# A decoder stack in float32: half of the second feed-forward matrix by Strassen's scheme, woven with tiles of the first

## The chip, the cores and the metric

The kernel runs on one NeuronCore of a Trainium2 chip. The metric is the device time of one execution in microseconds; the median of three runs of the kernel before is 2151.79 (2151.78 to 2152.73). TensorE (PE) multiplies, ScalarE (ACT) and VectorE (DVE) prepare operands and take results out of the accumulator banks (PSUM), GpSimd (POOL) and SyncE (SP) mostly issue transfers.

## The reference

Two hybrid attention layers, then one block of attention, convolution and feed-forward, on 256 rows of 2048, all in float32. The change concerns only the end of the last block:

```
f = rms_norm(h, g_ffn_pre)
f = square(relu(f @ w_ff1)) @ w_ff2      # w_ff1: 2048 x 8192, w_ff2: 8192 x 2048
h = h + rms_norm(f, g_ffn_post)
```

## The kernel before

Each float32 operand is split into a high part rounded to the matmul's float32r and a low part, the rest. A product is three matmuls: high by high, low by high, high by low. Weights come in blocks of 512 KB through a ring of four (`raw`, filled by SP); ScalarE rounds each block (`high`, L934, `round_block`) and VectorE subtracts (`low`, L490, `low_part`), `RING` blocks deep, so both work a few blocks ahead of TensorE.

TensorE's order is a numbered list of blocks made by `plan`: the feed-forward stage is 256 of them from `FF0` on. It has four quarters. A quarter is eight chunks `f1` of 256 hidden units (four blocks each, weights stationary, rows `xhl` moving, hidden tiles come out transposed) and then four chunks `f2` of 512 output columns (eight blocks each, hidden tiles stationary, weights moving). `weight_block` issues a block: eight matmuls of 512 and eight of 256 columns for `f1` (L682, L699), twelve of 512 for `f2` (L686, L687, L702). Two chunks use the four `acc` banks in turn.

ScalarE and VectorE run beside this by slots (`slots`, `ff_side`), a handful of tasks hung on block numbers. Of a finished `f1` chunk ScalarE copies the crossed half (L954, `cross_out`), VectorE adds it (L1300, `fold`), ScalarE takes relu, square and the rounded copy (L1242, L1244, L1246, `relu_square`), VectorE the low part (L1820). Of an `f2` chunk VectorE adds the banks into `mixed` (L1635, `ff_sum`). The squares of `x` that the norm of the rows needs (L1034, `squares`) hang on slots 10, 12, 14 and 16, two at a time.

The first two chunks of `f1` are interleaved block by block, since their rows are still being transposed (`h2T`, L606); L1792 makes the low part of those rows and counts `xt_ready`, 40 at the last. The last four blocks are done for one half of the rows and then the other, so that the norm of the first half runs under the second.

## Time and profile before

| | |
|---|---|
| median of three runs | 2151.79 us |
| the profiled execution, its span | 2150.6 us |
| around the span (median less span) | 1.2 us |
| TensorE busy | 2125.1 us (99%) |
| VectorE busy | 1361.9 us (63%) |
| ScalarE busy | 1106.1 us (51%) |
| mean granted TensorE clock | 0.999 of 2.4 GHz |

Busy time of matmuls is modelled and overlaps, so the time of a matmul is read from the distance between starts, not from its duration. The feed-forward stage takes about 710 us, a third of the span.

### The profile page before, as it was taken

To read this page: it belongs to the slowest core of one execution; us is meant where nothing else is said; L and a number is where in the kernel's file an instruction comes from. 1 tells how busy PE (TensorE), PEld (TensorE's weight loads), DVE (VectorE), ACT (ScalarE), POOL (GpSimd) and SP (SyncE) were. 2 spreads that over 40 slices of the span, in tenths; PEclk is the share of its full clock that TensorE was granted. 3 is DMA by queue.
4 is the path that set the end of the run, shared out by engine and by line. 5 is a ranking of instruction groups with operands and counts; after the bars stand their busy time and mean duration, and the time that the engine had idled before them with its cause. 6 is when DMAs were issued, how large, how long until landed. Compare 5 with 4: busy or idle time off the path is not lost. (4 is left out here: it accounts for less than half of the span.)

```text
span 2150.6 us, 29240 instructions
## 1 busy us (share of the span) xinstructions
PE 2125.1 (99%) x11602; PEld 1841.8 (86%) x11602; DVE 1361.9 (63%) x1979; ACT 1106.1 (51%) x1541; POOL 156.2 (7%) x78
## 2 busy tenths in 40 slices
PE   8999999999999999999999999999999999999998
PEld 7888888888988888888888888888888888888886
DVE  5554568875577558876578678766555555555555
ACT  4444554454464555555455455656435534544543
POOL 0000000000000000000007873000000000000000
PEclk9999999999999999999999999999999999999999
DMA  8666545655576655655656654646666666666664
GB/s 278 196 189 187 165 138 174 179 172 186 185 214 186 178 148 159 174 167 176 191 180 198 193 178 151 215 136 206 193 193 190 189 193 193 189 194 190 192 190 145
DMA packets 325031, 395.17 MB, mean 184 GB/s; under 512 B 20848, under 2 KB 252912, under 8 KB 324128
## 3 DMA queue, kind: packets, MB, share of 16 engines
q1 hardware_dynamic: 323104, 383.21, 59.0%
q0 software_dynamic: 1792, 10.10, 1.2%
q8 instruction: 92, 1.51, 0.3%
q14 instruction: 43, 0.35, 0.1%
HBM read 391.16 MB, written 2.10 MB: 183 GB/s over the span
## 5 line engine op out<-in xcount | busy, mean ns | idle before, releaser
L490 DVE TENSOR_TENSOR low<-raw,high 128x1024 fp32r<-128x1024 f32 (+2 forms) x672 | 809.9, 1209 | 639.0 <-ACT high L934 635.3
L934 ACT ACTIVATE high<-raw 128x1024 fp32r<-128x1024 f32 (+2 forms) x732 | 763.0, 1046 | 775.8 <-PE acc L682 201.7
L682 PE MATMUL acc<-xhl,high 128*128 128x512 f32 x3198 | 766.4, 391 | 0.0
L682 PEld LDWEIGHTS acc<-xhl,high 128*128 128x128 f32 x3198 | 587.0, 188 | 113.8 <-issue 0.7
L699 PE MATMUL acc<-xhl,low 128*128 128x256 f32 x3200 | 436.9, 286 | 1.9 <-DVE xhl L1792 1.4
L699 PEld LDWEIGHTS acc<-xhl,low 128*128 128x128 f32 x3200 | 414.4, 191 | 18.1 <-DVE xhl L1792 1.8
L686 PE MATMUL acc<-high,yhl 128*128 128x512 f32 (+1 forms) x1036 | 380.1, 373 | 2.2 <-DVE work L1718 1.6
L687 PE MATMUL acc<-high,yhl 128*128 128x512 f32 (+1 forms) x1036 | 378.8, 372 | 0.0
L702 PE MATMUL acc<-low,yhl 128*128 128x512 f32 (+1 forms) x1036 | 241.9, 374 | 0.2
L686 PEld LDWEIGHTS acc<-high,yhl 128*128 128x128 f32 x1036 | 195.2, 188 | 36.8 <-DVE work L1718 2.0
L687 PEld LDWEIGHTS acc<-high,yhl 128*128 128x128 f32 x1036 | 195.2, 188 | 33.8
L702 PEld LDWEIGHTS acc<-low,yhl 128*128 128x128 f32 x1036 | 182.9, 189 | 33.7 <-DVE yhl L1401 1.0
L490 POOL TENSOR_TENSOR low<-raw,high 128x1024 fp32r<-128x1024 f32 x61 | 147.9, 2437 | 81.2 <-ACT high L934 80.9
L1300 DVE TENSOR_TENSOR acc<-acc,cross 128x512 f32<-128x512 f32 x103 | 71.5, 694 | 37.2 <-ACT cross L954 37.0
L1682 DVE SCALAR_TENSOR_TENSOR tb<-work,params,tb 128x256 f32<-128x256 f32 x232 | 93.7, 480 | 0.0
L966 ACT ACTIVATE sc<-sc,small 128x128 f32<-128x128 f32 x64 | 28.6, 448 | 93.0 <-DVE small L1376 92.9
L686 PE MATMUL acc<-high,xhl 128*128 128x512 f32 (+2 forms) x224 | 73.7, 341 | 0.1
L687 PE MATMUL acc<-high,xhl 128*128 128x512 f32 (+2 forms) x224 | 73.1, 339 | 0.0
L702 PE MATMUL acc<-low,xhl 128*128 128x512 f32 (+2 forms) x320 | 72.7, 360 | 0.0
L954 ACT ACTIVATE cross<-acc 128x512 f32<-128x512 f32 x104 | 60.4, 581 | 1.9 <-PE acc L682 1.9
L702 PEld LDWEIGHTS acc<-low,xhl 128*128 128x128 f32 x320 | 53.7, 188 | 8.5 <-issue 1.3
L686 PEld LDWEIGHTS acc<-high,xhl 128*128 128x128 f32 x224 | 42.3, 189 | 5.2 <-issue 0.7
(228 smaller groups left out, 1286.9 us busy)
## 6 DMA issues: line engine op xcount, KB each, us to landing
raw<-in_w_in SPq DMA_DIRECT2D x328, 512.0 KB, 3.7
raw<-in_w_ff SPq DMA_DIRECT2D x256, 512.0 KB, 3.9
raw<-in_w_out SPq DMA_DIRECT2D x91, 512.0 KB, 4.3
raw<-in_w_mem_kv SPq DMA_DIRECT2D x32, 512.0 KB, 5.0
raw<-in_w_in SPq DMA_DIRECT2D x16, 256.0 KB, 2.7
raw<-in_w_out SPq DMA_DIRECT2D x10, 256.0 KB, 2.8
x_nat<-in_mem SPq DMA_DIRECT2D x4, 512.0 KB, 7.8
x_nat<-in_x POOLq DMA_DIRECT2D x4, 512.0 KB, 6.4
```

Of the source, the lines that this page charges most:

```text
L490: eng.tensor_tensor(part(low, g), part(raw, g), part(high, g).bitcast(F32), ALU.subtract).then_inc(ready, 1)
L682: ins = pe.matmul(acc[:, 2 * (c.acc % 2) + s, :], wh[:, t, at], vhl, start=first, stop=last)
L686: pe.matmul(outs[s], vh[:, at], wh[:, t, :], start=first, stop=False)
L687: ins = pe.matmul(outs[s], vl[:, at], wh[:, t, :], start=False, stop=last)
L699: ins = pe.matmul(acc[:, 2 * (c.acc % 2) + s, S:2 * S], wl[:, t, at], vh, start=crossed and t == 0, stop=last)
L702: ins = pe.matmul(outs[s], vh[:, at], wl[:, t, :], start=False, stop=last)
L934: act.activation(part(high, g), part(raw, g), ACT.Copy).then_inc(high_ready, 1)
L954: act.activation(cross, crosses(c), ACT.Copy).then_inc(cross_ready, 1)
L966: ins = act.activation(sc[:, j % 2, s, 0:n], src, ACT.Exp, bias=nmx[:, r:r + 1], accum_out=rs[:, r:r + 1])
L1300: dve.tensor_tensor(out, accs(c), cross, ALU.add).then_inc(folded, 1)
L1682: ins = dve.scalar_tensor_tensor(out=cv[:, ct, :] if tap == TAPS - 1 else sums_at, in0=src, scalar=w, in1=sums_at, op0=ALU.mult, op1=ALU.add)
```

## The change

The first 1024 of the 2048 columns of `w_ff2` are multiplied by Strassen's scheme in Winograd's form for 28 of the 32 pairs of hidden tiles: a pair (256 hidden units by 256 rows) and the matching 256 x 1024 weights are 2 x 2 blocks each, and seven products of 128 x 128 by 128 x 512 replace eight. The sums before it are made in float32 and then split in high and low: three sums of the weights (`group_sums`), four of the hidden tiles (`pair_sums`). A product keeps its own bank over four pairs (`RUNS` runs of four); then VectorE adds the seven banks to sums in memory (`sums_out`), and after the last run mixes these (`mix_sums`). The other 1024 columns, and all 2048 for the last four pairs, are taken in blocks as before (`piece`).

The first matrix is taken in 64 tiles of 128 hidden units, two blocks each (`feature_tile`), and the order is a new list, `FF_ORDER`: the high products of a group (14 matmuls), a tile, the low products (7), a tile; after four groups eight pieces. All seven product banks are busy, so every tile from the fifth on goes to the one bank `obank`, and ScalarE copies it out (`tile_copy`) before the next may start. VectorE folds, and takes relu and square in one operation of two halves (`relu_of`). Low parts of the blocks are written over the raw weights, so a load may start only when TensorE has used the block four before it. The groups' weights have two buffers of their own (`bset`), loaded by SP when the low products release them. The division by the row norm leaves the sum and appears in the last epsilon.

```diff
-    for q in range(NQ):
-        f1 = [("f1", q, j) for j in range(8)]
-        if q == 0:
-            run(*[chunk(k, a["w_ff1_2"][0], D * q + 256 * j, width=256, flipped=True) for j, k in enumerate(f1[:2])])
-        for j, k in enumerate(f1):
-            if q or j >= 2:
-                flip(k, a["w_ff1_2"][0], D * q + 256 * j)
-        for n, (col, width) in enumerate(FCOLS):
-            add(("f2", q, n), a["w_ff2_2"][0], col, width=width, row0=D * q)
+    w = a["w_ff1_2"][0]
+    run(*[chunk(("f1", 0, j), w, 256 * j, width=256, flipped=True) for j in range(2)])
+    w2 = a["w_ff2_2"][0]
+    for kind, *at in FF_ORDER:
+        if kind == "tile":
+            add(("g1", at[0]), w, P * at[0], width=P, nk=8)
+        elif kind == "piece":
+            e, n, i = at
+            if i == 0:
+                chunk(("f2", e, n), w2, CW * n, row0=8 * P * e, kts=8)
+            place(by["f2", e, n], i)
...
+TILES, TILES_AHEAD = 64, 4
+GROUPS, RUNS = 28, 7
+BESIDE = {0: (6, 7), 1: (None, 8), 2: (9, 10), 3: (None, 11)} | {j: (2 * j + 4, 2 * j + 5) for j in range(4, GROUPS)}
+def ff_order():
+    yield from (("tile", 4), ("tile", 5))
+    for j in range(GROUPS):
+        yield ("high", j)
+        if BESIDE[j][0] is not None:
+            yield ("tile", BESIDE[j][0])
+        yield ("low", j)
+        yield ("tile", BESIDE[j][1])
+        if j % 4 == 3:
+            yield from (("piece", j // 4, n, i) for n in (2, 3) for i in range(4))
+    for i in range(2):
+        for n in range(2):
+            yield ("piece", RUNS, n, i)
+            yield ("tile", 60 + 2 * i + n)
+    yield from (("piece", RUNS, n, i) for i in (2, 3) for n in range(2))
+    yield from (("piece", RUNS, n, i) for n in (2, 3) for i in range(4))
+FF_ORDER = list(ff_order())
+FF1 = FF0 + 8
...
+            def feature_tile(n):
+                if n > TILES_AHEAD + 1:
+                    pe.wait_ge(tile_out, n - TILES_AHEAD)
+                    if n - 12 in range(0, 56, 8):
+                        pe.wait_ge(piece_out, 4 * ((n - 12) // 8) + 3)
+                bank = tile_bank(n)
...
+            def group_high(j):
+                pe.wait_ge(pair_ready, j + 1)
+                pe.wait_ge(split_high, 3 * j + 3)
+                for p, unit, n in PRODUCTS:
+                    if j % 4 == 0:
+                        product_released(j // 4, p)
+                    for hl in range(2):
+                        pe.matmul(bank_of[p], rows_of(hl, j, n), bset_r[:, j % 2, 7 + unit, :], start=j % 4 == 0 and hl == 0,
+                                  stop=False)
+            def group_low(j):
+                pe.wait_ge(split_low, 3 * j + 3)
+                for p, unit, n in PRODUCTS:
+                    ins = pe.matmul(bank_of[p], rows_of(0, j, n), bset_r[:, j % 2, unit, :], start=False, stop=j % 4 == 3)
+                ins.then_inc(group_used, 1)
...
+            def tile_copy(n):
+                act.wait_ge(block_used, last_of(("g1", n)))
+                if n >= TILES_AHEAD + 2:
+                    act.wait_ge(pair_sq, n // 2)
+                act.activation(tcopy[:, n % 2, :], tile_bank(n), ACT.Copy).then_inc(tile_out, 1)
...
+            def ff_period(j):
+                n, b = next_blocks(j), BESIDE[j][0] is not None
+                p = {0: 2, 1: 3, 2: None, 3: 4}[j] if j < 4 else j + 1 if j % 4 else None
+                if j < 4 or j % 4:
+                    tile_copy(BESIDE[j - 1][1] if j else 5)
+                if b:
+                    round_block(n[2])
+                if j + 1 < GROUPS:
+                    split_h(j + 1, 0)
+                if b:
+                    round_block(n[3])
+                if j + 1 < GROUPS:
+                    split_h(j + 1, 1)
+                    split_h(j + 1, 2)
+                if b:
+                    tile_copy(BESIDE[j][0])
+                if p is not None:
+                    pair_h(p)
+                m = n[4:6] if b else n[2:4]
+                round_block(m[0])
+                round_block(m[1])
+                return m[1] + 1
...
+            cross_out(("f1", 0, 0))
+            round_block(FF1 + 2)
+            round_block(FF1 + 3)
+            cross_out(("f1", 0, 1))
+            split_h(0, 0)
+            pair_h(0)
+            split_h(0, 1)
+            split_h(0, 2)
+            round_block(FF1 + 4)
+            tile_copy(4)
+            round_block(FF1 + 5)
+            pair_h(1)
+            for c in range(4):
+                x_squares(c)
+            for j in range(GROUPS):
...
+            for b, task in enumerate((None, None, None, None, None, 60, None, None, 61, 30, None, None, 62, None, None, 63)):
+                if b >= 2:
+                    round_block(g + b)
+                if task in (60, 61, 62, 63):
+                    tile_copy(task)
+                if task == 63:
+                    pair_h(31)
+                if b == 10:
+                    pair_h(30)
...
+            def relu_of(pair, v):
+                if pair:
+                    dve.wait_ge(pair_ready, pair)
+                for t in range(2):
+                    ins = dve.scalar_tensor_tensor(out=combo[:, 2 * t:2 * t + 2, :].rearrange("p s n -> p (s n)"), in0=v[:, t], scalar=0.0,
+                                                   in1=v[:, t], op0=ALU.max, op1=ALU.mult)
+                ins.then_inc(pair_sq, 1)
...
+            def group_sums(g):
+                units = bset[:, g % 2]
+                dve.wait_ge(group_landed[g % 2][0], 16 * (g // 2 + 1))
+                dve.tensor_tensor(units[:, 1, :], units[:, 1, :], units[:, 0, :], ALU.subtract).then_inc(sum_step, 1)
+                dve.wait_ge(group_landed[g % 2][1], 16 * (g // 2 + 1))
+                dve.wait_ge(sum_step, 3 * g + 1)
+                dve.tensor_tensor(units[:, 4, :], units[:, 3, :], units[:, 1, :], ALU.subtract).then_inc(sum_step, 1)
+                dve.wait_ge(sum_step, 3 * g + 2)
+                t2 = units[:, 4, :].unsqueeze(1).broadcast_to([P, 2, CW])
+                dve.tensor_tensor(units[:, 5:7, :], t2, units[:, 0:3:2, :], ALU.subtract).then_inc(sum_step, 1)
+            def split_l(g, part_no):
+                dve.wait_ge(sum_step, 3 * g + 3)
+                dve.wait_ge(split_high, 3 * g + part_no + 1)
+                at, end = ((2, 4), (0, 2), (4, 7))[part_no]
+                dve.tensor_tensor(bset_r[:, g % 2, at:end, :], bset[:, g % 2, at:end, :], bset_r[:, g % 2, 7 + at:7 + end, :].bitcast(F32),
+                                  ALU.subtract).then_inc(split_low, 1)
...
+            def ff_period(j):
+                n, b = next_blocks(j), BESIDE[j][0] is not None
+                p = {0: 2, 1: 3, 2: None, 3: 4}[j] if j < 4 else j + 1 if j % 4 else None
+                if j == 3:
+                    fold_pair(p)
+                if j + 1 < GROUPS:
+                    group_sums(j + 1)
+                if p is not None and j != 3:
+                    fold_pair(p)
+                if b:
+                    low_block(n[2])
+                if p is not None and p < 4 * RUNS:
+                    pair_sums(p)
+                if b:
+                    low_block(n[3])
+                if j + 1 < GROUPS:
+                    for part_no in range(3):
+                        split_l(j + 1, part_no)
+                if j % 4 == 3:
+                    sums_out(j // 4, OUTS[:3])
+                if p is not None:
+                    pair_l(p)
+                m = n[4:6] if b else n[2:4]
+                low_block(m[0])
+                low_block(m[1])
+                return m[1] + 1
...
+            def piece_run(e, g):
+                p = 4 * e + 5
+                sums_out(e, OUTS[3:5])
+                low_block(g)
+                sums_out(e, OUTS[5:7])
+                fold_pair(p)
+                low_block(g + 1)
+                if p < 4 * RUNS:
+                    pair_sums(p)
+                low_block(g + 2)
+                pair_l(p)
+                low_block(g + 3)
+                pieces_out(e, 2)
+                for b in (4, 5, 6):
+                    low_block(g + b)
+                pieces_out(e, 3)
+                low_block(g + 7)
...
+            for b in range(2, 16):
+                low_block(g + b)
+                if b == 3:
+                    mix_sums()
+                if b == 9:
+                    fold_pair(30)
+                if b == 10:
+                    pair_l(30)
+            fold_pair(31)
+            pair_l(31)
...
+                if g >= FF1 + RING:
+                    sp.wait_ge(block_used, g - RING + 1)
...
+            def load_group(j):
+                if j < 2:
+                    sp.wait_ge(xt_ready, 40)
+                else:
+                    sp.wait_ge(group_used, j - 1)
+                for t in range(2):
+                    r0 = P * (2 * j + t)
+                    dst = bset[:, j % 2, 2 * t:2 * t + 2, :].rearrange("p a b -> p (a b)")
+                    sp.dma_start(dst, a["w_ff2_2"][0][r0:r0 + P, 0:2 * CW]).then_inc(group_landed[j % 2][t], 16)
```

ScalarE where the feed-forward stage begins, before: the crossed half of the second chunk, relu, square and rounding of the first, and the first squares of `x` between weight blocks.

```order
L954 ACTIVATE cross<-acc 128x512 [waits folded,block_used]
L934 ACTIVATE high<-raw 128x1024 [waits block_used,raw_landed1]
L1242 ACTIVATE cb<-acc 128x512 [waits folded]
L1244 ACTIVATE cb<-cb 128x512 [waits relu_ready]
L1246 ACTIVATE yhl<-cb 128x512 [waits fsq_ready]
L934 ACTIVATE high<-raw 128x1024 [waits block_used,raw_landed2]
L1034 ACTIVATE pt,small<-x_nat 128x512 [waits sq_ready,norm_ready]
L1034 ACTIVATE pt,small<-x_nat 128x512 [waits sq_ready]
L934 ACTIVATE high<-raw 128x1024 [waits block_used,raw_landed3]
```

The same engine at that place now: the copy of tile 4 (`tb`), a block, the high part of pair 1 and the first two of eight squares of `x`.

```order
L1465 ACTIVATE tcopy<-tb 128x512 [waits block_used]
L1144 ACTIVATE high<-raw 128x1024 [waits block_used,raw_landed2]
L1477 ACTIVATE hidden<-combo 128x2x512 [waits pair_step]
L1246 ACTIVATE ff_junk,small<-x_nat 128x512 [waits sq_ready,norm_ready]
L1246 ACTIVATE ff_junk,small<-x_nat 128x512 [waits sq_ready]
```

Six more squares follow, and then:

```order
L1465 ACTIVATE tcopy<-obank 128x512 [waits block_used]
L1144 ACTIVATE high<-raw 128x1024 [waits block_used,raw_landed3]
L1458 ACTIVATE bset_r<-bset 128x1024 [waits group_landed11]
L1144 ACTIVATE high<-raw 128x1024 [waits block_used,raw_landed0]
L1458 ACTIVATE bset_r<-bset 128x1024 [waits sum_step]
L1458 ACTIVATE bset_r<-bset 128x1536 [waits sum_step]
```

The first of these is the copy of tile 5 out of `obank`. The squares, two at a time between blocks before, now stand together ahead of the copy that frees the bank; the wait for tile 5 is all that it needs itself.

VectorE over one chunk of the first matrix before, in a later quarter:

```order
L1300 TENSOR_TENSOR acc<-acc,cross 128x2x256 [waits cross_ready]
L490 TENSOR_TENSOR low<-raw,high 128x1024 [waits high_ready] x2
L1820 TENSOR_TENSOR yhl<-cb,yhl 128x512 [waits yhi_ready]
L490 TENSOR_TENSOR low<-raw,high 128x1024 [waits high_ready] x2
L1300 TENSOR_TENSOR acc<-acc,cross 128x2x256 [waits cross_ready]
```

VectorE in the first part of a period now: sums of the next weight group, fold, relu-square, a block's low part, sums of the pair, another low part.

```order
L2109 TENSOR_TENSOR bset<-bset 128x512 [waits group_landed10]
L2112 TENSOR_TENSOR bset<-bset 128x512 [waits sum_step,group_landed11]
L2115 TENSOR_TENSOR bset<-bset 128x1024 [waits sum_step]
L2082 TENSOR_TENSOR tcopy<-tcopy 128x2x256 [waits tile_out]
L2075 SCALAR_TENSOR_TENSOR combo<-tcopy 128x256 [waits pair_ready,pair_fold]
L2075 SCALAR_TENSOR_TENSOR combo<-tcopy 128x256
L545 TENSOR_TENSOR raw_r<-raw,high 128x1024 [waits high_ready]
L2092 TENSOR_TENSOR combo<-combo 128x128 [waits pair_ready,pair_sq]
L2093 TENSOR_TENSOR combo<-combo 128x128
L2095 TENSOR_TENSOR combo<-combo 128x128 [waits pair_step]
L2097 TENSOR_TENSOR combo<-combo 128x128 [waits pair_step]
L545 TENSOR_TENSOR raw_r<-raw,high 128x1024 [waits high_ready]
```

Behind these come the three low parts of the weight group, that of the pair and two more blocks; where the queue held low parts and two small tasks for four blocks, it holds sixteen instructions.

TensorE in the first half of a period now: 14 high products and a tile, two blocks into `obank`.

```order
L873 MATMUL acc<-bset_r,hidden 128x512 [waits split_high,pair_ready]
L873 MATMUL acc<-bset_r,hidden 128x512 x3
L873 MATMUL sbank<-bset_r,hidden 128x512 x2
L873 MATMUL tb<-bset_r,hidden 128x512 x2
L873 MATMUL acc<-bset_r,hidden 128x512 x4
L873 MATMUL tb<-bset_r,hidden 128x512 x2
L835 MATMUL obank<-xhl,high 128x512 [waits high_ready,tile_out]
L835 MATMUL obank<-xhl,high 128x512 x7
L842 MATMUL obank<-xhl,raw_r 128x256 [waits low_ready]
L842 MATMUL obank<-xhl,raw_r 128x256 x7
L842 MATMUL obank<-xhl,raw_r 128x256 [waits low_ready]
L842 MATMUL obank<-xhl,raw_r 128x256 x7
```

Eight matmuls of 512 close the tile, and seven low products (which wait for `split_low`) and a second tile follow. The tiles wait for `tile_out`, ScalarE's copy of the tile before; the stretches of `f1` and `f2` blocks had no such products between them.

ScalarE and VectorE near the end: the copies of tiles 62 and 63 stand behind block roundings on ScalarE, and on VectorE the fold of the last pair stands behind five low parts, the last of which is that of the fourth block after tile 63.

```order
L1465 ACTIVATE tcopy<-obank 128x512 [waits pair_sq,block_used]
L1144 ACTIVATE high<-raw 128x1024 [waits block_used,raw_landed2]
L1144 ACTIVATE high<-raw 128x1024 [waits block_used,raw_landed3]
L1144 ACTIVATE high<-raw 128x1024 [waits block_used,raw_landed0]
L1465 ACTIVATE tcopy<-obank 128x512 [waits pair_sq,block_used]
L1477 ACTIVATE hidden<-combo 128x512 [waits block_used,pair_sq]
```

```order
L545 TENSOR_TENSOR raw_r<-raw,high 128x1024 [waits high_ready] x5
L2082 TENSOR_TENSOR tcopy<-tcopy 128x2x256 [waits tile_out]
L2075 SCALAR_TENSOR_TENSOR combo<-tcopy 128x256 [waits pair_ready,pair_fold]
L2075 SCALAR_TENSOR_TENSOR combo<-tcopy 128x256
L2102 TENSOR_TENSOR hidden<-combo,hidden 128x512 [waits pair_high]
L545 TENSOR_TENSOR raw_r<-raw,high 128x1024 [waits high_ready] x2
```

The high and low parts of pair 31 (`hidden<-combo`) are made there; before, the last chunk of a quarter was followed by seven blocks that did not use it.

## Rows read from the trace of the kernel before

**Rows 1.** The page, section 1: busy us and share of the span.

```profile
PE 2125.1 (99%) x11602; PEld 1841.8 (86%) x11602; DVE 1361.9 (63%) x1979; ACT 1106.1 (51%) x1541; POOL 156.2 (7%) x78
```

**Rows 2.** Busy time in an f1 and an f2 stretch; clock, DMA share, GB/s.

```profile
1790.00:1878.00 88.00, 88.00 (x509) 77.85 (x508) 48.68 (x48) 48.79 (x60) 0.00 (x0) 1.00 0.62 189
1878.00:1965.00 87.00, 87.00 (x386) 72.06 (x385) 44.28 (x41) 36.04 (x36) 0.00 (x0) 1.00 0.62 193
```

**Rows 3.** The chain in f1 and f2 blocks: start us, us, what.

```profile
1687.71 1.91 PE acc L699 x16
1689.63 3.65 PE acc L682 x16
...
1715.29 1.81 PE acc L702 x8
1720.73 1.81 PE acc L702 x8
```

**Rows 4.** Groups by shape, 1790 to 1965 us: busy us, mean ns.

```profile
L490 DVE TENSOR_TENSOR low<-raw,high 128x1024 fp32r<-128x1024 f32 x64 | 78.4, 1226 | 82.7 <-ACT high L934 82.7
L934 ACT ACTIVATE high<-raw 128x1024 fp32r<-128x1024 f32 x64 | 67.8, 1060 | 90.5 <-PE acc L702 26.3 <-PE acc L687 24.6 <-PE acc L699 23.9
...
L1246 ACT ACTIVATE yhl<-cb 128x512 fp32r<-128x512 f32 x8 | 5.1, 632 | 0.3
L1242 ACT ACTIVATE cb<-acc 128x512 f32<-128x512 f32 x8 | 4.6, 581 | 0.0
```

**Rows 5.** Timeline of VectorE before and at the stage: start us, us.

```profile
1419.53 0.69 DVE L490 TENSOR_TENSOR low<-raw,high 128x512 fp32r<-128x512 f32 x1
1420.14 0.68 DVE L1648 TENSOR_TENSOR work<-work,acc 128x512 f32<-128x512 f32 x1
...
1426.01 0.69 DVE L1648 TENSOR_TENSOR work<-work,acc 128x512 f32<-128x512 f32 x1 [0.72 <-PE acc L702]
1426.73 0.69 DVE L1657 TENSOR_TENSOR work<-work 128x512 f32<-128x512 f32 x1
...
1432.29 1.67 DVE L1792 SCALAR_TENSOR_TENSOR xhl<-tb,params,xhl 128x256 fp32r<-128x256 f32 x4 [0.90 <-ACT xhl L1228]
...
1452.91 0.88 DVE L1792 SCALAR_TENSOR_TENSOR xhl<-tb,params,xhl 128x256 fp32r<-128x256 f32 x2 [0.80 <-ACT xhl L1228]
1453.70 3.49 DVE L490 TENSOR_TENSOR low<-raw,high 128x1024 fp32r<-128x1024 f32 x3
```

**Rows 6.** Timeline of TensorE where the eight interleaved blocks end.

```profile
1457.69 3.82 PE L682 MATMUL acc<-xhl,high 128*128 128x512 f32 x16
```

**Rows 7.** Timeline of ScalarE: a rounding, and two squares of x.

```profile
1460.20 1.04 ACT L934 ACTIVATE high<-raw 128x1024 fp32r<-128x1024 f32 x1
...
1477.46 0.62 ACT L1034 ACTIVATE pt<-x_nat 128x512 f32<-128x512 f32 x1
1477.98 0.19 ACT L1034 ACTIVATION_READ_ACCUMULATOR pt<-x_nat 128x1 f32 x1
1478.19 0.63 ACT L1034 ACTIVATE pt<-x_nat 128x512 f32<-128x512 f32 x1
1478.73 0.18 ACT L1034 ACTIVATION_READ_ACCUMULATOR pt<-x_nat 128x1 f32 x1
```

**Rows 8.** DMA issues: KB each, median us to landing.

```profile
raw<-in_w_ff SPq DMA_DIRECT2D x256, 512.0 KB, 3.9
yf<-in_ln_gain POOLq DMA_DIRECT2D x2, 1024.0 KB, 4.6
```

**Rows 9.** Timeline of TensorE at the program's start.

```profile
6.38 1.94 PE L606 MATMUL tb<-consts,x_nat 128*128 128x128 f32 x8 [6.38 <-DMA x_nat<-in_mem]
...
10.77 3.48 PE L682 MATMUL acc<-yhl,high 128*128 128x512 f32 x8
14.09 1.11 PE L699 MATMUL acc<-yhl,low 128*128 128x256 f32 x8
...
19.51 2.07 PE L682 MATMUL acc<-yhl,high 128*128 128x512 f32 x8
```

437 lines of the change are left out of this document (327 added, 110 removed).

## Prediction

> **What bounds the kernel now.** I read the page first: TensorE is busy 99% of the span, VectorE 63%, ScalarE 51% [rows 1]. The feed-forward stage then split into stretches: over 88 us of first-matrix blocks and 87 us of second-matrix blocks TensorE is busy all of it at full granted clock, VectorE 55% and 51%, ScalarE 55% and 41%, the DMA engines 62% [rows 2]. Its waits are gone there, so matmuls alone price the stage. The chain gives their pitch. Two first-matrix blocks take 3.65 us (16 of 512 columns) and 1.91 us (16 of 256), so 0.228 and 0.119 us each; two second-matrix blocks are 5.44 us apart and hold 24 of 512 columns, 0.227 each [rows 3]. A block is 2.78 or 2.72 us.
>
> VectorE's own pitch matters next, since the change loads it. A low part of 1024 has a duration of 1.23 us [rows 4], but three in a row take 3.49, so the next starts after 1.14; 512 elements start 0.61 apart when free and 0.72 when one waits for the other; 256 come at 0.40 [rows 5].
>
> **What goes.** 28 pairs of hidden tiles by the first 1024 output columns need 7 products in place of 8, three matmuls each: 84 matmuls of 512 columns fewer, 84 x 0.227 = **-19.0 us**. Everything else on TensorE keeps count and shape. The products' 588 matmuls have a fresh stationary tile each and change bank as the old ones did, so I give them the same 0.227.
>
> **What VectorE and ScalarE get, steady state.** A period is one group (21 matmuls, 4.8 us) and two feature tiles (11.1): 15.9 us of TensorE. VectorE in it:
> - sums of the weight group: 512, 512, 1024, each waiting for the one before: 0.72 + 0.72 + 1.14 = 2.6
> - fold 0.72, relu-square two of 256 at 0.40: 1.5
> - four sums of 128x128: no such row. Below 0.2 each, above the 0.61 of a 512; near the 256 row, so 0.25: 1.0
> - four block lows 4.6; lows of the weight group 1024, 1024, 1536 (1.14 + 0.53): 4.0; low of the pair 1.1
>
> That is 14.7 to 14.8 us, 93% of the period. ScalarE: four roundings at 1.06, splits 1.06 + 1.06 + 1.5, two copies at 0.58, pair 1.06, together 10.1. DMA: 3 MB in 15.9 us, 198 GB/s against 189 to 193 now. Four periods, of which the first folds no pair and the last adds three sums, and a run of 8 pieces (21.8 us; VectorE 17.6): TensorE 85.3 us, VectorE 74.6.
>
> Busy share is not lateness, so I walked the deadlines. T is the start of a group's high products. Group weights were requested 5.6 us before T (the previous low products release the buffer) and 1 MB lands 4.6 us after a request [rows 8]; with a block load in between, about T, so VectorE begins there. Its splits end at T+11.4, its pair low at T+12.5; the next group's high products want the pair at T+15.9: 3.4 spare. ScalarE's copy of the first tile must fit into the low products' 1.6 us, because one PSUM bank holds every feature tile; it takes 0.58 and ScalarE's last split is done at about T+7.5, before the tile ends at T+8.7. The tightest place is the fourth piece: in a run's last period VectorE has 16.6 us of work up to the second piece's low (due at T+18.6), then four bank sums 2.4, a low 1.1, fold and square 1.5 and the fourth piece's low 1.1: T+22.8. That piece uses its low part first, at T+24.0. So 1.2 spare: steady state **0**. From below nothing can be gained, since TensorE cannot run ahead of its own matmuls; from above see the second rival.
>
> **The start.** Here I find a wait. Eight interleaved blocks end at 1457.69 + 8 x 0.228 = 1459.5 [rows 6]. TensorE then has four more feature blocks, to 1470.6. Behind it: the first group's load waits for the last transposed row tile, 1453.8 [rows 5], and stands ahead of two block loads in SP's queue, each worth 0.62 x 2.72 = 1.7 us of the DMA engines [rows 2, 3]. 1458.4, 1460.1, 1461.8 are the landings. Then in turn: ScalarE rounds the block 62.9, VectorE low 64.0, fold 64.6, four sums 65.7, ScalarE pair high 66.8, VectorE pair low 68.0, group sums 70.6, ScalarE's third split 72.1. The high products start 1.5 us late, and end at 75.3. Tile 6 needs the bank of tile 5, and its copy stands on ScalarE behind pair 1 and then eight squares of x, which before were spread two by two over the following slots. VectorE ends its splits at 74.5, a block low 75.7, square 76.5, sums 77.6; ScalarE pair high 78.7; squares 0.73 each (1.45 for two [rows 7]), 5.8 in all, 84.5; copy 85.1. TensorE waits from 75.3 to 85.2, 9.9. Start: 1.5 + 9.9 = **+11.4**. If the block loads land as before (rounding at 1460.2 [rows 7]) it is 10; if handshakes cost more, 14.
>
> After such an idle stretch the clock counts. At the program's start, after 6.38 us without work, eight 512-column matmuls took 3.48 us, later 2.07 [rows 9]: half speed for a few us. Bounds: 1.4 us (those eight) and 3.9 (half of all until 14.1); I take **+2.1**. The Trainium skill, "TensorE: Matmul & The Clock Gate", Part 1, has the same two levels, falling when TensorE idles and returning with sustained work; the trace's start agrees (3.48 against 2.07). Were it not to fall, the sum would be 2.1 lower.
>
> Groups 0 to 3 have six tiles beside them, not eight: TensorE 52.4 us, VectorE 53.1. VectorE enters the first pieces behind; walking on from 1485, the second piece waits 0.4 and the fourth 0.8: **+1.2** (bounds 0 and 3).
>
> **The end.** Tiles 60 to 63 alternate with pieces. The tile's copy stands behind the rounding of a block that was requested 2.78 before the tile's end: 3.9 + 1.06 + 0.6 against 5.5, some 0.2 for each of three: **+0.5**. Pair 31 is worse. From the end of tile 63 (U): block load U+3.8, rounding 4.9, VectorE low 6.1, and only then the fold 6.8, square 7.6, ScalarE 0.63 8.3, VectorE low 9.2. Two pieces cover 5.4: **+3.8** (bounds 2 and 5). The final normalisation is as before.
>
> **Sum.** -19.0 + 11.4 + 2.1 + 1.2 + 0.5 + 3.8 = 0.0. The profiled execution has a span of 2150.6, 1.2 below the median 2151.8, so the forecast stays at **2151.8**. Ends as bounded: start 10 to 14, clock 1.4 to 3.9, catch-up 0 to 3, end 2 to 5.5, together 13.4 to 26.4 against 19.0, so 2146 to 2159.
>
> **Rivals.**
> 1. Start and end cost less than I walked. For it: no row shows these handshakes at this density, and each of my durations includes one. All bounds at their low end give 13.4: 2146.2; without a fall of the clock 2144.8. Against: the eight squares are in ScalarE's order and cannot be passed.
> 2. VectorE becomes the bound in steady state. If each instruction costs its duration and not its pitch (+0.08), the 16 of a period make 16.0 in a period of 15.9, and the 30 from T to the fourth piece's low make that 2.4 later, less the 1.2 spare and with 0.2 carried over from the periods before: 1.4 in each of six runs, +8. With another 0.1 for each of the some 30 waits it is 4.4 a run, +26. I take it nearer to the row's own duration: +10, 2162. Against it: [rows 5] show the pitch where waits were already met. It decides once VectorE needs over 1.2 us more by the fourth piece.
> 3. Feature tiles are loaded in rows of 512 bytes, before 1 KB. 1 KB and 2 KB rows now load the engines equally (62% at 189 and 193 GB/s [rows 2]), so time goes by bytes. If a 512-byte row cost what 1 KB does, four blocks of a period would take 3.4 each and the group 3.4: 17.1 us, over 15.9; 1.2 x 28, less slack in the piece runs, +20: 2172. The Trainium skill, "DMA: Bandwidth & Descriptors", the table at its head, gives 512 B as the least transfer at full rate; no run here shows it yet.
> 4. The clock falls in the last wait too and stays low longer: +4, 2156 to 2158.
>
> Were the periods stall-free and both ends free, it would be 2132.8, but that needs the squares elsewhere.
>
> **Chances.** Start and end give the gain back (own range 2147.5 to 2156): 0.45. Rival 1: 0.2. Rival 2: 0.2. Rival 3: 0.08. Rival 4: 0.07. 0.2% of this kernel is 4.3 us, about what a measurement tells from no change. So faster 0.2, same 0.45, slower 0.35. The range 2145 to 2165 leaves out rival 3 and the far ends of 1 and 2.
>
> **What would show it.** TensorE idle of about 10 us before the second tile after the first group's high products, put down to ScalarE's copy; its next matmuls at twice the pitch; groups 15.9 us apart and runs 85.3; VectorE busy 88 to 95% between; a wait of 3 to 4 us before the pieces of the last pair. Wrong if waits for split_low or a block low recur in every run, if DMA share rises over 0.8, or if group matmuls have another pitch.

## The result: 1.4% slower, and the trace after

The changed kernel takes 2181.09 us (median of 4, 2180.84 to 2184.63) against 2152.26 (2151.78 to 2153.29) on the same chip: ratio 1.0136, 95% interval 1.0121 to 1.015. That is 29 us more than forecast and outside the range. The page of the changed kernel, section 1, as [rows 1] of before:

```profile
PE 2124.1 (97%) x11518; PEld 1834.0 (84%) x11518; DVE 1558.9 (72%) x2319; ACT 1129.2 (52%) x1534; POOL 161.0 (7%) x81
```

84 matmuls are gone, but TensorE's busy time only fell by 1.0 us, where 19 were due: what is left ran slower in places, and 29 us of waiting came on top. The list of waits of TensorE over the stage (1460 to 2170 us; us in total, times, longest):

```profile
PE obank L835 <- ACT tcopy L1465: 12.5, 6, 8.0
PE sbank L919 <- DVE raw_r L545: 6.8, 7, 2.0
PE acc L919 <- DVE hidden L2102: 4.5, 1, 4.5
PE acc L873 <- issue: 2.9, 1, 2.9
PE obank L919 <- DVE raw_r L545: 2.3, 1, 2.3
```

Two of these were not in my sum: 6.8 us in 7 waits for the low part of a second-matrix block, in each of runs 0 to 5, and 2.3 for the last of them. (Run 6 has none; in its last two periods no group is loaded, and in the last none is split.) ScalarE's list from 1562 to 2057 us, the first line of before and then of the changed kernel, shows what stands behind them:

```profile
ACT high L934 <- PE acc L699: 71.8, 48, 1.7
```

```profile
ACT high L1144 <- DMA raw<-in_w_ff: 165.7, 95, 4.6
```

Before, a rounding waited for TensorE to leave the slot of the rounded block: all four lines of that list name TensorE (253.8 us), and none a load. Now it waits for the block to land.

To compare kernels I cut the stage at the first high product of groups 0, 4 and 24 (TensorE's timeline): the start, then five whole runs, then the last run with the end, to the start of the last four matmuls. The first column is the time between groups 0 and 4. Medians are in us, "five slots" and the others are the kernels of the next section.

| kernel | 0 to 4 | five runs | last run, end | median |
|---|---|---|---|---|
| changed | 88.4 | 437.3 | 169.0 | 2181.1 |
| rows of 1 KB | 88.7 | 441.8 | 163.2 | 2180.5 |
| five slots | 87.6 | 429.0 | 151.5 | 2157.7 |
| squares later | 81.8 | 439.8 | 165.9 | 2174.6 |
| order at the end | 88.0 | 441.0 | 154.3 | 2172.2 |
| no group loads | 88.4 | 426.7 | 166.7 | 2167.3 |
| group load later | 88.6 | 435.9 | 165.1 | 2174.7 |
| 16 columns of sums | 86.7 | 431.9 | 165.1 | 2171.9 |
| all repairs | 78.5 | 428.6 | 150.5 | 2142.5 |
| all, 16 columns | 76.3 | 426.7 | 150.6 | 2138.7 |
| all but the start's order | 79.9 | 428.5 | 150.7 | 2148.7 |
| all, squares in the first run | 78.5 | 429.7 | 150.5 | 2142.7 |

A run without a wait lasts 85.33 us, all five of them in two of these kernels. My 85.3 for it was right, and with it the 0.227 for the new products. From it the first column would be 74.2 (two tiles, 11.1, less) and the third 150.2. So the changed kernel loses 3.1 (before group 0) + 14.2 = 17.3 at the start, 10.7 in the runs and 18.8 at the end, 46.8 in all; less 19.0 that is 27.8 of the 28.9 by which the spans differ (2179.5 and 2150.6). Of the other 1.1, 0.5 lie ahead of the first tile and 0.7 behind the last matmul, where the final normalisation takes 9.6 us for 8.9 before.

**One wait of a run, followed back.** TensorE, timeline in run 2:

```profile
1721.46 0.39 PE L919 MATMUL tb<-raw_r,hidden 128*128 128x512 f32 x1
1723.84 0.47 PE L919 MATMUL sbank<-raw_r,hidden 128*128 128x512 f32 x1 [2.00 <-DVE raw_r L545]
```

It waits for the low part of the fourth piece, which VectorE starts at 1722.48. VectorE (the low part at 1718.75 is the third piece's):

```profile
1715.93 0.68 DVE L2133 TENSOR_TENSOR m_b<-m_b,acc 128x512 f32<-128x512 f32 x1
1718.75 1.23 DVE L545 TENSOR_TENSOR raw_r<-raw,high 128x1024 fp32r<-128x1024 f32 x1 [2.14 <-ACT high L1144]
1719.89 0.68 DVE L2133 TENSOR_TENSOR m_b<-m_b,acc 128x512 f32<-128x512 f32 x1
1720.49 0.68 DVE L2133 TENSOR_TENSOR m_a<-m_a,acc 128x512 f32<-128x512 f32 x1
1721.09 0.68 DVE L2082 TENSOR_TENSOR tcopy<-tcopy 128x512 f32<-128x512 f32 x1
1721.80 0.76 DVE L2075 SCALAR_TENSOR_TENSOR combo<-tcopy 128x256 f32<-128x256 f32 x2
1722.48 1.22 DVE L545 TENSOR_TENSOR raw_r<-raw,high 128x1024 fp32r<-128x1024 f32 x1
```

VectorE stands idle for 2.14 us until the third piece's block has been rounded, and then has 2.6 us of sums, fold and squares ahead of the low part that is wanted: longer than the wait of 2.00 that follows. ScalarE, which rounds that block:

```profile
1717.65 1.06 ACT L1144 ACTIVATE high<-raw 128x1024 fp32r<-128x1024 f32 x1 [3.59 <-DMA raw<-in_w_ff]
```

and its load (the line's answer for 1709 to 1712 us):

```profile
L2315 SPq DMA_DIRECT2D raw<-in_w_ff x1: 379/379/379, 1710.7 to 1710.7; - x1
...
DMA to landing us min/median/max: 7.0/7.0/7.0
```

It was issued 2.8 us after the two halves of a weight group (1707.90, 1 MB) and took 7.0 us to land; 3.9 was the median of before [rows 8]. It could not be issued sooner: its slot holds the low part that TensorE had just used.

VectorE had come to these pieces late already. In the period before them (its high products start at T = 1697.4) it waited for both halves of the weight group:

```profile
1698.37 0.69 DVE L2109 TENSOR_TENSOR bset<-bset 128x512 f32<-128x512 f32 x1 [1.59 <-DMA bset<-in_w_ff]
1699.72 0.69 DVE L2112 TENSOR_TENSOR bset<-bset 128x512 f32<-128x512 f32 x1 [0.66 <-DMA bset<-in_w_ff]
```

They were issued 5.4 and 5.0 us ahead of T and took 6.3 and 7.3 us to land. The three sums ended at T+4.2; I had them end at T+2.6.

### The profile page after: what moved, and what is told of

The parts are those of the page before. It is cut to its first block and busy times, and to the rows that moved or that the text cites. A ratio compares the mean times of both kernels' runs of the same rounds, so it can differ in the third digit from the quotient of the medians.

```text
span 2179.5 us, 29676 instructions
## 1 busy us (share of the span) xinstructions
PE 2124.1 (97%) x11518; PEld 1834.0 (84%) x11518; DVE 1558.9 (72%) x2319; ACT 1129.2 (52%) x1534; POOL 161.0 (7%) x81
## 5 line engine op out<-in xcount | busy, mean ns | idle before, releaser
L545 DVE TENSOR_TENSOR low<-raw,high 128x1024 fp32r<-128x1024 f32 (+2 forms) x424 | 506.0, 1199 | 333.8 <-ACT high L1144 330.2
L775 PE MATMUL acc<-xhl,high 128*128 128x512 f32 x2238 | 537.0, 391 | 0.0
L775 PEld LDWEIGHTS acc<-xhl,high 128*128 128x128 f32 x2238 | 410.8, 188 | 79.5 <-issue 0.7
L792 PE MATMUL acc<-xhl,low 128*128 128x256 f32 x2240 | 312.4, 288 | 1.9 <-DVE xhl L2058 1.4
L545 DVE TENSOR_TENSOR raw_r<-raw,high 128x1024 fp32r<-128x1024 f32 x192 | 231.8, 1220 | 80.5 <-ACT high L1144 80.1
L835 PE MATMUL obank<-xhl,high 128*128 128x512 f32 x944 | 239.2, 396 | 12.5 <-ACT tcopy L1465 12.5
L835 PEld LDWEIGHTS obank<-xhl,high 128*128 128x128 f32 x944 | 175.1, 191 | 49.3 <-ACT tcopy L1465 15.5
L779 PE MATMUL acc<-high,yhl 128*128 128x512 f32 (+1 forms) x524 | 181.1, 358 | 2.1 <-DVE work L1984 1.6
L780 PE MATMUL acc<-high,yhl 128*128 128x512 f32 (+1 forms) x524 | 179.8, 356 | 0.0
L795 PE MATMUL acc<-low,yhl 128*128 128x512 f32 (+1 forms) x524 | 115.2, 360 | 0.2
L779 PEld LDWEIGHTS acc<-high,yhl 128*128 128x128 f32 x524 | 99.1, 189 | 16.9 <-DVE work L1984 2.0
L780 PEld LDWEIGHTS acc<-high,yhl 128*128 128x128 f32 x524 | 99.2, 189 | 13.8
```

Of the source, the lines that this page charges most:

```text
L545: eng.tensor_tensor(out, part(raw, g), part(high, g).bitcast(F32), ALU.subtract).then_inc(ready, 1)
L775: ins = pe.matmul(acc[:, 2 * (c.acc % 2) + s, :], wh[:, t, at], vhl, start=first, stop=last)
L779: pe.matmul(outs[s], vh[:, at], wh[:, t, :], start=first, stop=False)
L780: ins = pe.matmul(outs[s], vl[:, at], wh[:, t, :], start=False, stop=last)
L792: ins = pe.matmul(acc[:, 2 * (c.acc % 2) + s, S:2 * S], wl[:, t, at], vh, start=crossed and t == 0, stop=last)
L795: ins = pe.matmul(outs[s], vh[:, at], wl[:, t, :], start=False, stop=last)
```

## Experiments

Theory A: the low part in place of the raw block shortens the lead of every load to three blocks (8.3 us). Theory B, my own rival 2: VectorE has too much work. C: the group loads crowd the block loads. D: the short lead alone. E: the rows of 512 bytes.

**Five slots.** 1024 words a partition are free in the old low ring; they take a fifth raw block.

```diff
                 if g >= FF1 + RING:
-                    sp.wait_ge(block_used, g - RING + 1)
+                    sp.wait_ge(block_used, g - RING)
...
-                        if g + RING < BLOCKS:
-                            load_block(g + RING)
+                        if g + 5 < BLOCKS:
+                            load_block(g + 5)
```

> The changed kernel with five slots for raw weight blocks in place of four in this stage (the fifth lies in memory that is free there); nothing else is changed. Theory A (short lead): since the low part is now written over the raw block, a load must wait until TensorE has used the block four before, where it used to wait only for VectorE; landing 4.3, rounding 1.06 and low part 1.2 then leave under 2 us of the 8.3, and any wait of TensorE stops the loads too. It expects ScalarE's waits for the raw block to fall from 244 us to under 60, runs 1 to 5 to last 85.3 to 86 instead of 86.2 to 90.1 (9 us), and at the end the copies of tiles 60 to 62 and the low part before the last rows to be in time, with the slow matmuls behind them (about 10 us): 2158 to 2164. Theory B (VectorE has too much work in a run): the waits of 0.9 to 2.0 us in the runs stay, the time falls by less than 10, to 2172 to 2181, by what the end gives alone.

2157.66 us, ratio 1.0023 (1.0013 to 1.0033): 23.4 less for one slot. Its waits of TensorE, 1460 to 2170 us:

```profile
PE obank L842 <- ACT tcopy L1475: 8.0, 1, 8.0
PE acc L880 <- issue: 3.1, 1, 3.1
PE sbank L926 <- DVE raw_r L552: 1.3, 4, 0.3
PE acc L926 <- DVE hidden L2112: 0.9, 1, 0.9
PE sbank L926 <- DVE raw_re L552: 0.4, 1, 0.4
```

The waits of the runs are 0.3 each instead of up to 2.0; the three late copies and the last low part are gone, the last pair's wait fell from 4.5 to 0.9. ScalarE's waits for blocks fell from 242 to 103 us, not under 60. The start is as it was. A holds (the time is 0.3 below its range); for B 0.3 a run is left, and VectorE still waits for the weight groups there (37.9 us from 1562 to 2057), so with the fifth slot a late group costs no more than that.

**No group loads.**

```diff
-                if kind == "low" and at[0] + 2 < GROUPS:
-                    load_group(at[0] + 2)
...
+            for j in range(2, GROUPS):
+                pool.wait_ge(group_used, j - 1)
+                for t in range(2):
+                    pool.memset(bset[:, j % 2, 2 * t:2 * t + 2, :].rearrange("p a b -> p (a b)"), 0.0).then_inc(group_landed[j % 2][t], 16)
```

> The changed kernel with the weight groups from the third on not loaded: GpSimd writes zeros in their place (their products are left out of the result that way), all other instructions stay. That takes 1 MB in each period off the DMA engines. Theory C (the groups' loads, 6.7 us to landing, crowd the block loads): block loads land in under 4 us, runs lose their waits, the time falls by 8 to 12, to 2169 to 2173. Theory A: the blocks that come late in a run are asked for when no group is loaded, so the waits of the runs stay and the time is within 4 us of 2181, unless GpSimd's writes slow VectorE.

2167.26 us, 13.8 less, 1.7 below C's range. Four slots, and no wait in runs 1 to 5. Block loads from 1562 to 2057 us landed in 4.0 (median) and 4.9 at most, in the changed kernel in 4.3 and 7.5. C holds, and my reading of A, that the late block is asked for when no group is loaded, was wrong: the load shown above had 1 MB ahead of it. The waits at both ends stay (9.5, 4.6, 2.7, 1.8). The zeros also stand ready when VectorE wants them, so this run takes away the group's own lateness together with the crowding; how the two share the 10.7 us it does not tell.

**In-place low parts in the kernel before.** The one part of the change alone.

```diff
-            eng.tensor_tensor(part(low, g), part(raw, g), part(high, g).bitcast(F32), ALU.subtract).then_inc(ready, 1)
+            eng.tensor_tensor(part(rawr if g >= FF0 + 8 else low, g), part(raw, g), part(high, g).bitcast(F32), ALU.subtract).then_inc(ready, 1)
...
-                if g >= RING:
+                if g >= FF0 + 8 + RING:
+                    sp.wait_ge(block_used, g - RING + 1)
+                elif g >= RING:
```

> The kernel before, with one part of the change alone: in the feed-forward stage the low part is written over the raw block, so a load waits until TensorE has used the block four before, no longer for VectorE. No weight groups, no Strassen products, nothing else moved. Theory D (the short lead alone is what costs): waits in the middle of the stage as in the changed kernel, 2160 or more. Theory A with C (the short lead costs only where a block load stands behind a group load of 1 MB): landing 3.8, rounding 1.06 and low part 1.2 are 6.1 of 8.3 us, so no wait in the middle; at the very end four half blocks last 5.4, a wait of about 1 with some slow matmuls behind it: 2152 to 2155.

2156.54 us, ratio 1.0018 (1.0009 to 1.0027). ScalarE's waits from 1500 to 2057 us, and TensorE's one wait after the transposes:

```profile
ACT high L936 <- DMA raw<-in_w_ff: 282.9, 179, 3.4
```

```profile
2136.94 0.73 PE L704 MATMUL acc<-raw_r,yhl 128*128 128x512 f32 x2 [2.07 <-DVE raw_r L492]
```

ScalarE waits for 179 blocks, and still TensorE for none until the last four, where half blocks follow each other in 1.4 us. D falls: by itself the short lead costs 4.0 us by the medians (2.2 by the spans), 1.5 above the range I gave, with a wait of 2.07 where I expected 1, much as at the end of the changed kernel (2.33).

**The group load moved.** From the last period of a run to the middle of its pieces.

```diff
-                if kind == "low" and at[0] + 2 < GROUPS:
+                if kind == "low" and at[0] % 4 != 3 and at[0] + 2 < GROUPS:
                     load_group(at[0] + 2)
+                if kind == "piece" and at[0] + 1 < RUNS and at[1:] == [2, 3]:
+                    load_group(4 * at[0] + 5)
```

> The changed kernel with one thing moved in the DMA queue: the group load that was issued in the last period of each run, 2.8 us ahead of the run's first late block load, is issued in the middle of the run's eight pieces. Slots and waits stay. In the changed kernel the block load behind it took 7.0 us to land and the next 5.4, against 3.8 without groups. Theory A with C (short lead and a group load ahead of a block load): runs 1 to 5 last 85.3 to 85.7, the waits before piece lows of 0.9 to 2.0 fall to 0.3 or less, 9 to 10 us less in all: 2170 to 2173. Theory B (VectorE's volume in the run): the waits stay, time within 3 us of 2181. Theory D (the short lead alone): the same as B.

2174.69 us; a miss. The five runs take 435.9, 1.4 less and not 9 to 10. The wait of 2.00 in run 2 is 0.35, but new ones of 0.8 to 1.5 stand at a later piece in runs 1, 3, 4 and 5: in run 2 the blocks around the group load landed in 4.6 and 5.8 us. Of the two places tried for the megabyte neither is much better; any eight blocks without group products between them have the bare 8.3 us of lead. The other 5 us less lie outside the runs, 3.9 of them at the end, where this kernel and the changed one are the same, so that is the spread between executions: the stretches of slow matmuls behind its last three long waits are 3.5 us together here and 6.8 there.

**Sums of 16 columns**, four slots.

```diff
-                    dve.tensor_tensor(sum_of[p], sum_of[p], bank_of[p], ALU.add).then_inc(out_step, 1)
+                    dve.tensor_tensor(sum_of[p][:, 0:16], sum_of[p][:, 0:16], bank_of[p][:, 0:16], ALU.add).then_inc(out_step, 1)
```

> The changed kernel as it is, four slots and all, but VectorE adds only 16 of the 512 columns of each of the seven product sums of a run (the rest is left out). Theory A with C holds that the run's first block, behind a group load, lands 7.0 us after its request and reaches VectorE at 1718.75, where it stands idle for 2.14; behind it come two sums, fold and squares of 3.7 us, and then the low part that TensorE waits for. With the two sums gone that comes some 1.0 us sooner, so of a wait of 2.0 about 0.9 stays: 3 to 6 us less in all, 2175 to 2178. Theory B alone (VectorE's volume): all those waits go, 10 or more less, under 2172. Neither: within 2 of 2181.

2171.86 us. VectorE in run 2:

```profile
1714.84 1.22 DVE L545 TENSOR_TENSOR raw_r<-raw,high 128x1024 fp32r<-128x1024 f32 x1 [4.04 <-ACT high L1144]
1715.98 0.16 DVE L2133 TENSOR_TENSOR m_b<-m_b,acc 128x16 f32<-128x16 f32 x1
1716.06 0.16 DVE L2133 TENSOR_TENSOR m_a<-m_a,acc 128x16 f32<-128x16 f32 x1
1716.14 0.69 DVE L2082 TENSOR_TENSOR tcopy<-tcopy 128x512 f32<-128x512 f32 x1
1716.86 0.76 DVE L2075 SCALAR_TENSOR_TENSOR combo<-tcopy 128x256 f32<-128x256 f32 x2
1717.54 1.22 DVE L545 TENSOR_TENSOR raw_r<-raw,high 128x1024 fp32r<-128x1024 f32 x1
```

VectorE does less and waits more (4.04), and TensorE's wait in run 2 is 0.77, in runs 4 and 5 0.98 and 0.97: the 0.9 that A with C gave. The total is 3 us below my range; 3.9 us of the 9.2 lie in the last run and the end, where the changed kernel has no wait that these sums are part of, and where the slow matmuls are 3.5 us in place of 6.8, as when the group load was moved. So the wait of 2.0 is a sum: a landing 3 us late, and the sums, fold and squares placed between two low parts.

**All repairs, with the sums whole and with 16 columns.** "All" is five slots, squares later, order at the end (below) and another order at the start. The second kernel has the edit above too.

```diff
-            low_block(FF1 + 2)
-            low_block(FF1 + 3)
-            fold(("f1", 0, 1))
             pair_sums(0)
-            pair_l(0)
             group_sums(0)
-            for part_no in range(3):
-                split_l(0, part_no)
-            low_block(FF1 + 4)
+            pair_l(0)
+            low_block(FF1 + 2)
+            low_block(FF1 + 3)
+            fold(("f1", 0, 1))
             dve.wait_ge(folded, flip_no(by["f1", 0, 1]) + 1)
             relu_of(1, cross)
             pair_sums(1)
+            low_block(FF1 + 4)
+            for part_no in range(3):
+                split_l(0, part_no)
...
```

ScalarE's order at the start is changed to match.

> All repairs together: five raw slots, the squares of x behind the first four periods, the order at the end, and at the start another order: ScalarE and VectorE take pair 0 and the sums of the first weight group in the time in which both waited for a block (1459 to 1463), and the splits after that. From 2157.7 with five slots alone, the waits of 3.1 and 8.0 at the start and the about 4.4 us of slow matmuls behind them should go, and the 0.9 of the last pair: 2141 to 2145, faster than before. If VectorE is too full at the start (rival), up to 5 of it stays: 2146 to 2149.

> All repairs, and VectorE adds only 16 of the 512 columns of each of the seven product sums of a run (the rest is left out, so the result lacks them): some 3.5 us less of VectorE's work in each run, nothing else. Theory B in what is left of it: the waits of 0.3 to 0.6 before a piece's low part in runs 0, 2 and 4 (2.2 in all) are VectorE's and go, 2139.5 to 2141.5. If they are still there, they come from landings.

2142.46 us, ratio 0.9955 (0.994 to 0.997): faster than before. With 16 columns 2138.68 (0.8 below the range), and the waits for low parts (0.3 to 0.6) are gone. This is what is left of rival 2: VectorE's load costs 0 to 1.0 a run, 2.0 over five, and 2.2 at the start.

**Squares later.**

```diff
-            for c in range(4):
-                x_squares(c)
             for j in range(GROUPS):
                 g = ff_period(j)
+                if j < 4:
+                    x_squares(j)
...
-                if j == 0:
+                if j == 4:
                     dve.wait_ge(sq_ready, 16 + 2 * NC)
```

> The changed kernel with the eight squares of x put behind the first four periods, two behind each, in place of all before the first; VectorE reads their sum one run later. All theories expect the wait of 7.98 us before tile 6 to fall to about 2 (the copy of tile 5 then stands behind pair 1 alone), and with it part of the 3 us that slow matmuls cost there: 2172 to 2176. If the clock's loss belongs to the waits ahead of it (the first high products), only 5 to 6 us come back: 2175.

2174.55 us. The wait before tile 6 fell from 7.98 to 1.93.

**Order at the end.**

```diff
-            for b, task in enumerate((None, None, None, None, None, 60, None, None, 61, 30, None, None, 62, None, None, 63)):
+            for b, task in enumerate((None, None, None, None, 60, None, None, 61, None, None, 62, None, None, 63, None, None)):
...
-            fold_pair(31)
-            pair_l(31)
+                if b == 13:
+                    fold_pair(31)
+                    pair_l(31)
```

> The changed kernel with another order at the end alone: ScalarE copies tiles 60 to 63 one block earlier (62 and 63 two), ahead of the rounding whose load is asked for when the tile ends, and VectorE folds and squares the last two pairs as soon as the copies are there, ahead of the low parts. Waits there now: 0.41, 0.45, 3.00 for copies, 4.53 for the last pair, and about 6.5 us of slow matmuls behind them. Theory A expects them all to go and the wait of 2.33 for the low part before the last rows, with its 1.6 of slow matmuls, to stay: 2166 to 2170. Theory B, where VectorE's work sets the last pair: the copies' waits go, that of the pair stays at 3 or more: 2173 to 2176.

2172.21 us. The end took 14.7 less: the four waits are gone, that for the last low part stays at 2.10, as A had it, and B's 3 us for the pair are not there. The total is 2 us above the range, and the profiled execution 1.1: three of its runs waited 1.9 each and had 1.7 of slow matmuls behind it, where the changed kernel's profile had that in one.

**Rows of 1 KB.**

```diff
+                if c.name[0] == "g1" and g >= FF1 + RING:
...
+                    sp.dma_start(raw[:, g % RING, :].rearrange("p (t n) -> p t n", t=4),
+                                 c.w[r0:r0 + 4 * P, col:col + 256].rearrange("(t p) n -> p t n", p=P)).then_inc(raw_landed[g % RING], 16)
```

> The changed kernel with each feature tile's block loaded as 4 x 128 rows of 1 KB in place of 8 x 128 rows of 512 bytes: the same bytes into the same place, from other rows of the matrix, so those products are others than the reference's. Theory E (rows of 512 bytes load the DMA engines more): block loads land sooner than 3.8, the DMA share falls well under 0.64, and the time by 5 us or more. The others: landing within 0.2 of before, waits and time the same, 2178 to 2184.

2180.5 us, the same. E falls. The windows from 1562 to 2057 us, of this kernel and then of the changed one (the last two columns are the DMA share and GB/s):

```profile
1562.00:2057.00 495.00, 483.55 (x2457) 410.98 (x2456) 415.28 (x508) 260.18 (x271) 0.00 (x0) 1.00 0.61 189
```

```profile
1562.00:2057.00 495.00, 488.44 (x2488) 416.07 (x2487) 416.80 (x509) 261.54 (x273) 0.00 (x0) 1.00 0.64 190
```

0.61 against 0.64 at the same rate: 5%, and nothing in the time. Block loads landed in 3.9 (median, 8.2 at most) for 4.3 and 7.5, sooner by more than the 0.2 I had allowed the other theories; the waits and the time stayed. The Trainium skill, "DMA: Bandwidth & Descriptors", the table at its head, has 512 B as the least transfer at full rate; this pair agrees as far as its 190 GB/s go.

**All but the start's order, and the squares in the first run.** Two small ones.

> Five raw slots, the squares behind the first four periods and the order at the end, but the start in the changed kernel's own order. It prices that order: against 2142.5 with all repairs the wait for the first group's splits (3 us) and the slow high products behind it (about 1.7) are there again, and the copy of tile 5 stands behind pair 1 (2): 2147 to 2150.

2148.69 us, so the start's order is worth 6.2; with the changed kernel's start it is still 0.19% faster than before (ratio 0.9981, 0.9972 to 0.999).

> All repairs, but the squares of x stand among the roundings of the first run's last four pieces, where ScalarE has 1.6 us to spare for each, and not behind the first four periods. The two waits of 0.55 and 0.44 for a tile's copy in the first periods should go: 2140.5 to 2142.5, at the edge of what can be measured. If those waits are not the squares', no change.

2142.74 us, no change: of the two waits the 0.5 before tile 6 stays, which cannot be the squares'; the other is gone, too small to measure.

## Why the prediction was wrong, step by step

- **What goes, -19.0.** Right. A run without waits is 85.33 us, forecast 85.3. What I had wrong is "the final normalisation is as before": from the last matmul to the end it is 0.7 us longer in the changed kernel, and 11.1 for 8.9 in the one with all repairs, which no run explains.
- **Steady state 0: the step that failed.** Measured 10.7 in five runs; waits for a block's low part in one run after another were my own sign of being wrong. The place was right: the fourth piece, due at T+24.0, had its low part forecast for T+22.8. In run 2 T is 1697.4 (15.9 ahead of the first piece at 1713.27), and the low part ended at 1723.7, T+26.3. Of the 3.5 us, 2.14 are VectorE's idle time for the third block; the other 1.4 it was already late when it ended the second piece's low part (1715.4, T+18.0 for T+16.6), and that alone uses up the 1.2 to spare, as the 0.3 a run with five slots shows. The 1.4 is the weight group's: landed at T+1.0 and T+2.3 for my T. I had walked VectorE's work and taken each block as landed. But a block's load had got a new condition (TensorE's use of the block four before) and a new neighbour (1 MB of group weights), and took 7.0. I had the 3.9 of [rows 8], and the 4.6 beside it, for loads of before, where no megabyte lay on the queue ahead of them; I used them for the group and at the end, never for the blocks of a run. The 4.6 was also the quickest of four kinds of 1 MB load in the same list of before; the others took 5.1, 6.7 and 8.2, and a group's half 6.7 in the median:

```profile
yf<-in_ln_bias POOLq DMA_DIRECT2D x2, 1024.0 KB, 6.7
```

  Fewer group bytes, one slot more, or fewer VectorE instructions there each take most of it away.
- **VectorE's load.** Close: once the blocks are in time, taking its sums away gives only 2.0 us in five runs. Rival 2 (+10) did not happen: that the runs lost 10.7 is chance, since its cause, VectorE's volume alone, is not what cost it. A wait "for VectorE" stood in six of seven runs all the same, which I had named as its sign. The sign was too weak: it tells only who came last.
- **The start, 11.4 + 2.1 + 1.2 = 14.7.** Measured 17.3. The mechanism was right. TensorE's timeline:

```profile
1474.23 1.31 PE L873 MATMUL acc<-bset_r,hidden 128*128 128x512 f32 x4 [2.94 <-issue]
...
1478.64 0.61 PE L873 MATMUL tb<-bset_r,hidden 128*128 128x512 f32 x2
1487.24 3.78 PE L835 MATMUL obank<-xhl,high 128*128 128x512 f32 x8 [7.98 <-ACT tcopy L1465]
1490.82 2.67 PE L842 MATMUL obank<-xhl,raw_r 128*128 128x256 f32 x16
1493.32 2.00 PE L835 MATMUL obank<-xhl,high 128*128 128x512 f32 x8
```

  The first products were 3.1 late, not 1.5, so the wait for the copy was 8.0, not 9.9; together 11.1 for 11.4. The eight matmuls took 3.78 (twice the pitch) and the next sixteen 2.67 for 1.9, some 2.4 for my 2.1. Not in the sum: the slow high products after the first wait, 1.7. The rest is 0.9 in the first pieces (1.2 forecast) and slow matmuls behind them.
- **The end, 0.5 + 3.8 = 4.3: the term furthest off.** Measured 18.8. The last pair's wait was 4.53 for 3.8. Tile 62's copy I had behind "a block that was requested 2.78 before the tile's end". ScalarE:

```profile
2112.95 1.06 ACT L1144 ACTIVATE high<-raw 128x1024 fp32r<-128x1024 f32 x1 [1.69 <-DMA raw<-in_w_ff]
2115.87 1.06 ACT L1144 ACTIVATE high<-raw 128x1024 fp32r<-128x1024 f32 x1 [1.86 <-DMA raw<-in_w_ff]
2116.83 0.58 ACT L1465 ACTIVATE tcopy<-obank 128x512 f32<-128x512 f32 x1
```

  The tile ended at 2111.58. For it one more rounding stands ahead than for tiles 60 and 61, of a block requested when the tile ended: 3.00 for 0.2. I read the order of two tiles and took the third as alike, though the list of tasks in the diff has tile 62 four roundings behind tile 61, where 61 is three behind 60. The last low part (2.33) is the short lead again, unseen. The other 8.1 are, all but some 1, slow matmuls (2.9 behind the wait of 3.00, 2.3 behind 4.53, 1.6 behind 2.33), which I priced at the start alone. Windows behind the waits for tile 6, the copy and the pair (granted clock third from the end):

```profile
1487.20:1494.00 6.80, 6.76 (x27) 5.89 (x28) 6.71 (x11) 5.14 (x5) 0.00 (x0) 0.64 0.02 6
...
2117.40:2125.00 7.60, 7.54 (x28) 6.63 (x29) 2.01 (x2) 1.07 (x2) 0.00 (x0) 0.59 0.13 35
...
2136.00:2143.00 7.00, 6.94 (x21) 5.58 (x22) 3.66 (x5) 1.29 (x2) 0.00 (x0) 0.66 0.08 25
```

  The DMA share is 0.02 to 0.13 in the same windows: when TensorE had stood still, no load had been issued. Rival 4 named this fall for the last wait and gave it +4; at the end it came behind three waits and took 6.8.
- **In all.** 14.5 of the 27.8 us are from the end, 10.7 from the runs, 2.6 from the start. Of the end 17.5 and of the runs 8.3 went with one raw slot: one unpriced change, the release of the slot, has a part in most of the miss. It is not the whole cause: alone, in the kernel before, it cost 4.0; in the runs it needed the megabyte ahead (no loss without it), and at the end the order of the copies (14.7 less with another). Other executions differ by some 4 to 6 us: the same order at the end took 163 to 169, and the same runs 437 to 442. Much of that is whether the clock falls behind a wait, as the last section shows.

## What to carry to other kernels

When a buffer is reused in place, walk its release: what the next load now waits for, how many blocks of lead that leaves, and which larger load stands ahead of it in the queue when it is issued. A wait "for VectorE" is to be followed back until an engine is found that was busy all the time; here it ended at a DMA. One slot of 512 KB was worth 23 us, more than the 84 matmuls saved, and the saving only showed when the waits at both ends were cut as well (2142.5 us, 0.45% faster than before).

## What the runs showed of the hardware

A 512 KB load issued 2.8 us behind 1 MB took 7.0 us to land, the next 5.4, and without the megabyte 3.7 to 4.9. Waits of TensorE can cost more than they last: in the changed kernel behind 2.00 us came 1.7 of slow matmuls, behind 2.33 1.6, behind 3.00 2.9, behind 4.53 2.3 and behind 7.98 2.4, at granted clocks down to 0.59 in the windows above, which is a mix of 2.4 and 1.2 GHz; the Trainium skill, "TensorE: Matmul & The Clock Gate", Part 1, has these two levels. For a wait of about 2 us it is a toss: of the 21 waits of 1.8 to 2.4 us in all traces here (from 1460 us on), 9 were followed by 1.6 to 1.7 us of slow matmuls and 12 by 0.1 ("rows of 1 KB" waited 1.98 to 2.00 in four runs, and one of them paid). Of the 28 waits of 2.6 us and more 26 cost another 1.4 to 2.9, and of those of 0.9 to 1.6 none more than 0.1.
